# Attention block: places of three sets of squares, of one wait of TensorE and of the last cross rounds

## The reference

```python
h = rmsnorm(x, g_mix[l])                       # x: 512 x 1024
dq, dk, dv, c_q, c_kv_kr, xq, gate_logits = split(h @ w_in[l])
# differential attention: 8 heads, 2 maps of width 64 each, values of width 128
q = rotary(rmsnorm(q, q_gain)); k = rotary(rmsnorm(k, k_gain))
o = softmax(q0 k0^T) v - lam * softmax(q1 k1^T) v
o = rmsnorm(o, out_gain) * (1.0 - lam_init)    # over the 128 columns of a head
# latent attention (MLA): 8 heads, q and k of width 96, v of width 64
q = rmsnorm(concat([q_nope, rotary(q_rope)]), q_gain)
k = rmsnorm(concat([k_nope, k_rope]), k_gain)
# cross attention: 4 heads of width 128 against 256 rows of memory
merged = gates[0]*y_diff + gates[1]*y_mla + gates[2]*y_mem
x = x + merged @ w_out[l]
x = x + square(relu(rmsnorm(x, g_mlp[l]) @ w_mlp1[l])) @ w_mlp2[l]
```

## Time and profile before

| | |
|---|---|
| median of three executions | 2820.3 us |
| profiled execution, whole | 2820.44 us |
| its span, first to last instruction | 2818.6 us |
| PE busy | 2633.5 us, 93% |
| POOL busy | 1871.9 us, 66% |
| DVE busy | 1109.6 us, 39% |
| ACT busy | 786.3 us, 28% |
| mean granted clock of TensorE | 0.97 |

### The profile page before, as it was taken

One profiled execution on the slowest core, in us unless ns is written; L12 is line 12 of the kernel. 1 busy time (PEld: TensorE's weight loads), 2 busy tenths in 40 slices (PEclk: granted clock), 3 DMA queues, 4 the chain that ended last, 5 costly groups with the idle time before them and its releaser, 6 DMA issues. The chain is left out here.

```text
span 2818.6 us, 36007 instructions
## 1 busy us (share of the span) xinstructions
PE 2633.5 (93%) x13720; PEld 2121.8 (75%) x13724; DVE 1109.6 (39%) x1836; ACT 786.3 (28%) x1589; POOL 1871.9 (66%) x1554
## 2 busy tenths in 40 slices
PE   5999889999999999999889999999998997989797
PEld 4888566877878887888666878888887974688655
DVE  3544665211221112444566211210102488526983
ACT  4332474100120112242474100120111233314251
POOL 4647513888898888747523888898886871367604
PEclk9999899999999999999899999999999997999989
DMA  4322101333333333322201233333334330043202
GB/s 135 96 56 78 44 8 32 87 94 91 105 94 98 94 97 113 96 62 73 57 8 27 83 94 97 89 94 98 94 97 87 98 83 23 31 91 90 72 1 75
DMA packets 159259, 214.51 MB, mean 76 GB/s; under 512 B 51696, under 2 KB 69360, under 8 KB 159088
## 3 DMA queue, kind: packets, MB, share of 16 engines
q1 hardware_dynamic: 120336, 207.27, 25.6%
q10 hardware_dynamic: 38752, 4.95, 1.4%
HBM read 210.06 MB, written 2.10 MB: 75 GB/s over the span
## 5 line engine op out<-in xcount | busy, mean ns | idle before, releaser
L369 POOL TENSOR_TENSOR weight_parts<-weight_ring,zero 128x512 fp32r<-128x512 f32 (+4 forms) x730 | 789.9, 1082 | 729.9 <-PE ps L458 367.4
L372 POOL TENSOR_TENSOR weight_parts<-weight_ring,weight_parts 128x512 fp32r<-128x512 f32 (+3 forms) x804 | 1064.6, 1324 | 135.9 <-ACT weight_parts L380 77.8
L460 PE MATMUL ps<-h_feature_major_high,weight_parts 128*128 128x512 f32 x2304 | 590.5, 394 | 12.2 <-POOL weight_parts L369 11.6
L460 PEld LDWEIGHTS ps<-h_feature_major_high,weight_parts 128*128 128x128 f32 x2304 | 428.0, 188 | 119.9 <-POOL weight_parts L369 19.3
L458 PE MATMUL ps<-weight_parts,h_feature_major_high 128*128 128x512 f32 (+3 forms) x1904 | 431.1, 364 | 22.8 <-POOL weight_parts L369 8.9
L458 PEld LDWEIGHTS ps<-weight_parts,h_feature_major_high 128*128 128x128 f32 x1904 | 334.2, 190 | 76.7 <-POOL weight_parts L369 10.7
L460 PE MATMUL ps<-h_feature_major_low,weight_parts 128*128 128x512 f32 x1152 | 309.7, 391 | 0.0
L458 PE MATMUL ps<-weight_parts,ut_high 128*128 128x512 f32 x1008 | 251.6, 390 | 1.1 <-POOL weight_parts L369 1.0
L460 PEld LDWEIGHTS ps<-h_feature_major_low,weight_parts 128*128 128x128 f32 x1152 | 217.3, 189 | 46.4
L634 PE MATMUL ps<-arena 64*128 64x512 f32 (+9 forms) x704 | 176.8, 505 | 78.7 <-ACT probs L751 60.9
L458 PE MATMUL ps<-weight_parts,h_feature_major_low 128*128 128x512 f32 (+3 forms) x952 | 227.6, 361 | 0.0
(11 more groups left out here) (281 smaller groups left out, 3006.4 us busy)
## 6 DMA issues: line engine op xcount, KB each, us to landing
weight_ring<-in_w_in SPq DMA_DIRECT2D x272, 256.0 KB, 2.6
weight_ring<-in_w_mlp SPq DMA_DIRECT2D x256, 256.0 KB, 2.6
weight_ring<-in_w_out SPq DMA_DIRECT2D x64, 256.0 KB, 2.6
weight_ring<-in_w_mem_kv SPq DMA_DIRECT2D x32, 256.0 KB, 2.7
weight_ring<-in_w_diff_o SPq DMA_DIRECT2D x32, 256.0 KB, 2.6
weight_ring<-in_w_in SPq DMA_DIRECT2D x32, 170.0 KB, 2.3
weight_ring<-in_w_in SPq DMA_DIRECT2D x32, 168.0 KB, 2.2
weight_ring<-in_w_in SPq DMA_DIRECT2D x32, 163.0 KB, 2.2
```

What stands on the lines that cost most here:

```text
L369: self.nc.gpsimd.tensor_tensor(high, raw, self.m["zero"][:].broadcast_to([P, raw.shape[1]]), ALU.add).then_inc(self.s["slab_high"], 1)
L372: self.nc.gpsimd.tensor_tensor(low, raw, high.bitcast(F32), ALU.subtract).then_inc(self.s["slab_split"], 1)
L460: last = self.nc.tensor.matmul(banks[:, t, :], w[:, cut], h, **ends)
```

## The change

- MLA's two pieces of squares of k, the mean, the square root and the reciprocals run before the differential attention instead of in its rounds. ScalarE's square root now stands ahead of its copy of dv1, followed by one exponential of a single column (`warm`), which brings the exponentials' table in.
- The squares and sums of the differential outputs run after the last differential unit and before the first MLA unit, in free columns of `arena`.
- `attend` waits for the last group's copy ahead of the fourth round instead of after the first, in all three attentions.
- dk1's squares are no longer taken from PSUM before the copy, but from the copy, after round 3 of the cross attention.
- The last three cross rounds stand after slabs 0, 2 and 4 of lat0 instead of 0, 1 and 2.

```diff
+            "warm": sb("warm", [P, 1]),
...
-    def attend(self, pe, A, lo, hi, before_turns=None, projection=None, finished=None):
+    def attend(self, pe, A, lo, hi, before_turns=None, projection=None, finished=None, every=1):
...
         for i in range(lo, hi + 1):
+            if i == lo + 3:
+                self.emptied(pe, max(self.last, key=self.order.index))
             A.round(i, lo, hi, parts, ahead)
-            if i == lo:
-                self.emptied(pe, max(self.last, key=self.order.index))
...
-            self.project(pe, *projection, {1 + k: f for k, f in enumerate(tail)})
+            self.project(pe, *projection, {1 + every * k: f for k, f in enumerate(tail)})
...
-            L.attend(pe, A, 0, U1, ("dk1", ht), ("lat0", ht))
+            L.attend(pe, A, 0, U1, ("dk1", ht), ("lat0", ht), every=2)
...
+            def square_last():
+                act.wait_ge(s["squares_used"], squares[0])
+                squares[0] += 1
+                a.activation(sq[:, 0:TT * W512].rearrange("p (t n) -> p t n", t=TT), qk[:, :, 3 * W512:],
+                             ACT.Square).then_inc(s["squares"], 1)
...
             full(act, "dk1")
-            square("dk1")
             empty("dk1", qk[:, :, 3 * W512:])
-            A.steps(0, U1, (3, A.copy), (0, A.exp), ahead=2)
+            A.steps(0, U1, (3, A.copy), (0, A.exp), ahead=2, between={3: square_last})
...
+            roots(st_both)
+            a.activation(m["warm"][:], m["zero"][:], ACT.Exp)
             empty("dv1", dv[:, :, W512:])
...
-            A.steps(U1, U2, (3, A.copy), (0, A.exp), (4, round_out), between={prep_rounds[-2]: lambda: roots(st_both)})
+            A.steps(U1, U2, (3, A.copy), (0, A.exp), (4, round_out))
...
             L.emptied(dve, "kvb1")
-            A.steps(U1, U2, (0, A.maximum), (1, A.scale), between=dict(zip(prep_rounds, pieces)))
+            for t in range(0, TT, 2):
+                square_mla(t, 1)
+            mean_mla()
+            rstd_mla()
+            A.steps(U1, U2, (0, A.maximum), (1, A.scale))
+
+            squared = view(arena, 16384, TT, D)
+            dve.wait_ge(s["finished"], U2)
+            for t in range(TT):
+                v.tensor_tensor(squared[:, t, :], od[:, t, :], od[:, t, :], ALU.mult)
+                v.drain()
+                v.tensor_reduce(st_o[:, t, :], squared[:, t, :].rearrange("p (h d) -> p h d", h=DH), AX.X, ALU.add)
...
-            for t in range(TT):
-                w = sq_late[:, 0:1024]
-                dve.wait_ge(s["turned"], U3)
-                v.tensor_tensor(w, od[:, t, :], od[:, t, :], ALU.mult)
-                v.drain()
-                v.tensor_reduce(st_o[:, t, :], w.rearrange("p (h d) -> p h d", h=DH), AX.X, ALU.add)
-                v.drain()
             rstd(st_o, [(st_o, P)])
```

5 lines of the change are left out of this document (removed).

## The result

The changed kernel takes 2785.1 us (median of 4 runs, 2783.9 to 2785.8), the kernel before 2822.1 (median of 4, 2819.9 to 2824.7): ratio 0.9868, 95% interval 0.9856 to 0.988. The profiled execution has a span of 2784.0 us against 2818.6.

The account below looks back on a forecast made before the run. Bound: TensorE, with waits and low clock between slab stages. A layer 10.3 - 2.1 + 2.0 + 0.4 = 10.6, two 21.2, plus 0.3 cross: 21.5 us, so 2799 us; forecast 2793 to 2806, 2789 to 2810 8 times in 10.

Parts of the forecast that it names:

- MLA's attention: Second MLA unit's scores no longer wait 1.94 us for the turned k's last copy: 2.0 us a layer, ends 0 and 2.3.
- the cross attention: Cross attention to lat1, both layers: 4.85 us gained less 4.6 for low clock, so 0.3 gained; ends -8 and +8.
- The differential attention: Seven heads: of 14.3 us excess a layer, 5.25 stay (3.75 GpSimd's scaling, 1.5 clock) and 9.05 go.
- The slabs of dv1: Slabs of dv1: two more VectorE products beside GpSimd's splitting lose 2.1 us a layer.
- The start of the differential rounds: First differential rounds: moved wait and earlier table load start them 1.25 us sooner a layer.
- Behind it: Behind MLA's attention: the large product runs earlier but its stall stays; 0.4 us a layer, ends -0.5 and +5.
- The lead: Cross attention: lat0 begins 4.8 us earlier in layer 0, 3.45 in layer 1.
- the price of the distance: Last cross unit two slabs later: VectorE's fourth rotation chain begins 3.7 us later against lat0's start.
- 1 (the disturbance only moves): First differential rounds: GpSimd's scaling now disturbs these; 9 us of excess stay, not 5.25; 2806 to 2811, chance 0.16.
- Rival 2: Lat1 and large product: no clock fall behind TensorE's wait, product's stall gone or halved; 2787 to 2793 us, chance 0.13.
- Rival 3: Early differential rounds: slow for another reason, such as pipeline fill; only the starts gain; 2812 to 2820 us, chance 0.04.
- Rival 4: Ahead of dv1's copy: ScalarE's root waits for a late VectorE chain, delaying everything behind; slower, chance 0.03.

Follow-up runs that it names:

- Without the scaling: GpSimd's scaling of MLA's q and k cut to one column of each head: 2817.1 us on the kernel before, 2782.4 us on the changed kernel.
- the scales alone: Kernel before with only k's squares, mean and reciprocals ahead of the differential rounds, root and warm exponential ahead of dv1's copy: 2796.6 us.
- the cut product: Changed kernel with the last cross rounds behind every chunk of lat0 and VectorE's large product of the outputs cut into four: 2770.2 us.
- the rounds in every chunk: Changed kernel with the last three cross rounds behind every chunk of lat0, as before, not every second: 2777.6 us.

## Why the prediction was wrong

The sum had 21.5 us, the trace 34.6. The 13 us between them come from the seven heads (6.6), the stretch behind gate00 (3.2), MLA's attention (2.8) and the part behind both layers (4.2), less 3.4 in the cross attention and 0.2 at the start of the rounds. By its own steps:

1. **The differential attention kept too little of its excess: right mechanism, size off.** "I keep 3.75" for GpSimd's scaling and "1.5 for the clock" was wrong; 16.4 us for this stage with the slabs of dv1 became 22.8. Of the 5.25 us kept a layer above 53.6, 2.6 and 1.3 were there. The failing step is the reading of "the three heads from 342.59 to 370.19 took 27.6 instead of 23.0, 4.6 us more" as GpSimd's price. Without the scaling these heads took 24.7, so it costs 2.9 us before, and 0.8 to 2.0 after; the other 1.7 us stay without it and so belong to what stands in front, most likely the recovery from the root, whose low clock reached past 342 (eight matmuls in 1.91 us at 344.27, where 1.06 is full speed). The 1.5 us for the clock were too much as well: 0.5 to 0.7 us above 53.6 are left in the changed kernel without the scaling. I cut the excess by the clock on the wall, not by what caused it.
2. **The slabs of dv1, 2.1 us, were right** (2.3 with the scales alone; in the changed kernel's layer 0 dv1 took 26.92 us up to the first scores, against 24.55). The two added waits and the four GpSimd pieces of 2.56 us came as read from the earlier trace rows.
3. **The start of the differential rounds, 1.25 us, was right, but it is a gain only with the scales ahead.** dv1 to the first scores is 1.4 us shorter with the moved wait. With the wait alone, the seven heads gave it back (69.4). From dv1 to the eighth scores the scales alone took 83.6 us; the changed kernel took 83.8 in layer 0, with its spell of the low clock, and 82.4 in layer 1.
4. **MLA's attention, 2.0 us a layer with 2.3 as its end, became 3.4.** I priced the wait (2.1 us less) and not the low clock behind it, which stood a few rows further on (four matmuls in 2.54 us, where 1.53 is the full speed).
5. **Behind it, 0.4 us a layer became 2.5 and 1.5.** "That the eight operations in front of it are gone from here gains nothing else, as TensorE did not wait for them" was wrong. They had delayed GpSimd's low parts (2.36, 2.17 and 2.16 us), so GpSimd came late to the piece that the large product holds up: TensorE had 1.8 us of slabs left then, and 2.6 in the changed kernel. With the piece itself 0.35 us shorter (4.87 for 5.22) this is the 1.1 us of the stall. The output squares alone gave the shorter stall. Most of the rest is clock: an estimated 2.4 us of low clock in layer 0's stage before, 1.6 after.
6. **The cross attention, +0.3, became -3.1, within its ends.** The lead was right (4.4 and 3.5 us for 4.8 and 3.45), and so was the price of the distance, 3.65 for 3.7. The 2.0 us of less contention did not come: GpSimd, slowed by the same chain, split until 218.9, and the chain kept its 16.05 us. TensorE's wait grew to 8.38 us and not 4.6 for this and because the slabs ahead of it were done 21.3 us after lat0's start, against 24.7 before; what they gained, the wait took. The clock's 2.3 a layer was 1.6 and 2.2.
7. **4.2 us came from where nothing was counted**, behind layer 1. The moved wait reaches the second block's attention too, which calls the same `attend` (the description of the change has it in the first block only), and I had not priced it. But that stretch took 1257.2 to 1261.9 us among the five kernels with the old wait, whose instructions there are the same, and 1257.3 to 1264.1 among those with the new one: no effect of the edit can be read from it. The kernel before has the longest but one. What sets it is open: the low clock has other lengths there from trace to trace (780 to 840 us behind layer 1's outputs 0.70 in the kernel before, 0.72 in the changed one, 0.66 with the output squares alone), and no run was made on it. Without these 4.2 us the median would stand at 2789.3, just inside the range; the other misses alone would have left the forecast of 2793 to 2806 but not the range.

The rivals: 1 (the disturbance only moves) fell with a seven-head time of 56.2 us, below the 59 expected. Rival 2 named the side on which it came out, but not the cause: the clock did fall behind the 8.38 us, and the gain came mostly from the rounds. Rival 3 (the early rounds are slow for another reason) fell with the gain of the scales alone. Rival 4 did not occur, as ScalarE's root was done 8 us ahead. Of the rule that a VectorE instruction with two inputs in SBUF and a GpSimd instruction that reads SBUF exclude each other for a whole instruction (the Trainium skill, "SBUF — State Buffer", Who interferes with whom), the cut product is the plainest test here: GpSimd's piece fell from 4.87 to 1.67 us when VectorE's instruction was cut to a quarter, so the trace agrees that the unit of waiting is an instruction.

## What to carry to other kernels

When an excess in a stage is shared out among causes, share it by taking a cause away in one run, or at least by the row at which each recovers; a neighbour in time is not a cause. Read behind each wait of TensorE the next few rows for the half clock, and price wait and clock together. A long chain behind the last round of a stage can be worth moving between the rounds (17 us here, where the spacing of the rounds was worth 7.5), and an instruction that holds another engine up can be worth cutting, though it gets slower itself.

## What was not expected of the hardware

- The same wait in the same place had different sequels. Behind that of 217.77 with the rounds in every chunk TensorE ran its 16 turns in 3.01 us, and turn to dv1 took 70.7 us. The kernel with the cut product has the same program up to there, and TensorE's waits before its turns are the same to 0.01 us (0.34, 0.80, 0.35, 0.89 and 0.28 us from 207.93 on). But TensorE kept the full clock there (granted clock in the 4 us from the turns: 1.00 against 0.59), and turn to dv1 took 69.1. The same step lies between the kernel before (221.94) and that with the output squares alone. First the cut product's turns, then those with the output squares alone:

```profile
217.22 1.97 PE L484 MATMUL ps<-ident,arena 128*128 128x128 f32 x16 [1.34 <-DVEq L1429]
```

```profile
221.18 3.01 PE L483 MATMUL ps<-ident,arena 128*128 128x128 f32 x16 [1.34 <-DVEq L1424]
```

So neither the length of the wait nor what TensorE did in the microseconds before it decides alone; what else does, these traces don't show. The stretch behind gate00 has two lengths behind the same stall of 2.35 us (34.2 and 35.8), and MLA's attention has them too (58.0 and up to 60.1 with the old wait, 54.65 and 55.95 with the new). A stage read from one trace can be off by 1.3 to 2 us for this reason, with no edit behind it.

- Four VectorE products of 128x1024 beside GpSimd took 7.42 us, 1.86 each, while one of 128x4096 took 4.43. Cutting the one shifted the cost from GpSimd (4.87 to 1.67 us for its piece) to VectorE.
- A table load of 1.28 us had the exponential straight behind it (335.56 and 336.85), so a root between rounds stops ScalarE's exponentials for 3.0 us. In the stage it cost more than that, by the estimate above 4 to 6.5 us.
